# A hybrid attention, state-space and gated-FFN block on one Trainium2 core: the GLU chain rewritten, loads of u split, lists around the down phase reordered

## The reference, cut to what matters

```python
h = rms_norm(x, norm_mix)
q, k, v, u, g = split(h @ w_in)               # 512 | 128 | 128 | 512 | 2 x 1024
a = window_attention(q, k, v, sinks, bias) @ w_attn_branch
y = gelu(Re(C state) + D u)                   # grouped S5 scan over u, 32 groups
b = (y * sigmoid(y @ w_glu + b_glu)) @ w_ssm_branch
x = x + (sigmoid(g_a) * a + sigmoid(g_b) * b) @ w_out
h = rms_norm(x, norm_ffn)
val, gate = split(causal_dwconv(h @ w_up) + conv_b)   # 2 x 2816 columns
x = x + (gelu(gate) * val) @ w_down
return rms_norm(x, norm_final)
```

## Time and profile before

| | |
|---|---|
| time, median of 3 | 2474.99 us |
| the profiled execution | 2474.55 us, span 2472.8 us |
| PE | busy 98% of the span |
| DVE, POOL, ACT | busy 70%, 35%, 30% |
| mean granted TensorE clock | 0.992 of full speed |
| chain that ended last | PE 90%, DVE 5%, DMA 2%, ACT 2%, issue 1% |
| DMA | 367.35 MB, 149 GB/s in the mean |

### The profile page before, as it was taken

How to read it: one execution, slowest core, us unless ns; L and a number is a source line. 1 busy time by engine, 2 the same in 40 slices (tenths; PEclk the granted TensorE clock), 3 DMA queues, 4 the chain that set the end, 5 groups by cost and what they waited for, 6 DMA issues and landing times.

```text
span 2472.8 us, 33390 instructions
## 1 busy us (share of the span) xinstructions
PE 2417.0 (98%) x11578; PEld 1980.7 (80%) x11578; DVE 1737.5 (70%) x2585; ACT 746.4 (30%) x1431; POOL 855.5 (35%) x689
## 2 busy tenths in 40 slices
PE   7999999999999999999999999999999999999997
PEld 6887777888788888788878877778878888888886
DVE  6964564546899999989750346466378888888896
ACT  4145113212333333332221341132133333333222
POOL 2421222450455555623232222235213333334231
PEclk9999999999999999999999999999999999999999
DMA  6266553351334334698522536534312222218863
GB/s 206 77 182 108 175 170 120 133 194 71 102 126 156 135 131 133 216 371 290 183 88 90 104 119 188 158 105 156 148 60 80 91 85 76 78 75 289 311 230 136
DMA packets 178279, 367.35 MB, mean 149 GB/s; under 512 B 22344, under 2 KB 60008, under 8 KB 178168
## 3 DMA queue, kind: packets, MB, share of 16 engines
q1 hardware_dynamic: 135568, 278.23, 34.7%
q10 hardware_dynamic: 42600, 87.64, 10.3%
HBM read 277.20 MB, written 88.60 MB: 148 GB/s over the span
## 4 chain that ended last, share of the span: by engine, by line
PE 90%; DVE 5%; DMA 2%; ACT 2%; issue 1%; POOL 0%; ACTq 0%; SPq 0%; DVEq 0%; POOLq 0%
PE ps L497 28%; PE ps L499 28%; PE ps L498 28%; DMA gates<-junk 1%; PE ps L2220 1%; PE ps L2222 1%; PE ps L2202 1%; DVE ybr_lo L1681 1%; PE ps L2026 1%; PE ps L2074 0%; PE ps L2159 0%; DVE glu_y L1676 0%; ACT ybr_hi L909 0%; DVE z L1809 0%; DVE act_lo L1842 0%
## 5 line engine op out<-in xcount | busy, mean ns | idle before, releaser
L839 POOL CAST slot_hi<-pair_raw 128x512 fp32r<-128x512 f32 x220 | 201.7, 924 | 394.4 <-PE ps L499 305.5
L497 PE MATMUL ps<-act_hi,w_hi 128*128 128x512 f32 x832 | 332.1, 399 | 1.5 <-issue 1.5
L499 PE MATMUL ps<-act_hi,w_lo 128*128 128x512 f32 x832 | 325.4, 391 | 0.0
L498 PE MATMUL ps<-act_lo,w_hi 128*128 128x512 f32 x832 | 324.6, 390 | 0.0
L793 POOL CAST w_hi<-w_raw 128x1024 fp32r<-128x1024 f32 x72 | 80.6, 1119 | 678.4 <-PE ps L499 668.8
L497 PE MATMUL ps<-act_hi,slot_hi 128*128 128x512 f32 x704 | 274.4, 390 | 1.8 <-DVE pre L1795 1.5
L499 PE MATMUL ps<-act_hi,slot_lo 128*128 128x512 f32 x704 | 274.0, 389 | 0.0
L498 PE MATMUL ps<-act_lo,slot_hi 128*128 128x512 f32 x704 | 273.9, 389 | 0.0
L497 PE MATMUL ps<-act_hi 128*128 128x512 f32 x616 | 242.0, 393 | 3.2 <-DVE act_lo L1846 3.2
L498 PE MATMUL ps<-act_lo,act_hi 128*128 128x512 f32 x616 | 240.9, 391 | 0.0
L499 PE MATMUL ps<-act_hi,act_lo 128*128 128x512 f32 x616 | 240.8, 391 | 0.0
(11 more groups left out here) (325 smaller groups left out, 4953.2 us busy)
## 6 DMA issues: line engine op xcount, KB each, us to landing
w_raw<-in_wu SPq DMA_DIRECT2D x88, 512.0 KB, 3.4
pair_raw<-in_wu SPq DMA_DIRECT2D x88, 512.0 KB, 4.1
step_f<-ff SPq DMA_DIRECT2D x88, 512.0 KB, 5.2
ff<-z SPq DMA_DIRECT2D x44, 512.0 KB, 2.6
gates<-junk ACTq DMA_DIRECT2D x64, 256.0 KB, 2.1
sig<-gates ACTq DMA_DIRECT2D x32, 512.0 KB, 5.3
tbl_o<-tables ACTq DMA_DIRECT2D x32, 384.0 KB, 3.6
step_w<-in_wu SPq DMA_DIRECT2D x22, 512.0 KB, 6.8
```

The lines of the kernel that those rows point to most:

```text
L497: nc.tensor.matmul(out, lh, rh, start=first, stop=False, skip_group_check=onto)
L498: nc.tensor.matmul(out, lh, rl, start=False, stop=False, skip_group_check=onto)
L499: return nc.tensor.matmul(out, ll, rh, start=False, stop=last, skip_group_check=onto)
L839: nc.gpsimd.tensor_copy(slot_hi[j][:, :, :], src).then_inc(slot_half[KIND[j]], 1)
```

## The change: what it does

1. GLU: `yT_lo` goes to 160 KiB, where the S5 tables lay, and `ybr_lo` to 112, over `yT`. The value is read from `yT` itself, so the sum (L1674, sixteen in all) is gone. The sigmoid waits for the product that read its buffer, not for `ybr_lo`. All four `y_low` stand behind the last S5 step. The buffers `wo` of the output weights change places to fit.
2. Loads of u: three, three and two transfers, with a pair of weight units behind each group; in block 1 the first group goes ahead of units 14 and 15 and behind 13, in block 0 likewise ahead of 14 and 15.
3. Start of the down phase: DVE interleaves `step_lows` 2, 3, 4 with `near`, `far` and `ff_mul` of the last value; ACT casts step 3 ahead of the last gelu; POOL's last `down_t` stands behind cast 4 instead of cast 2; the last value's store stands ahead of load 10 instead of load 7, and there SP waits for it at once, as before.
4. Between the blocks: in block 0 `bank_add` stands ahead of `out_scaled`; the four output stores move behind the second projection half of block 1; the transposes of the second x half stand ahead of the second product, all but the last two.
5. PE asks for `ybr_lo` before each of the first two S5 products of the merge instead of before the first.

```diff
-        yT_lo = at("yT_lo", 112, [4, T], F32R)
+        yT_lo = at("yT_lo", 160, [4, T], F32R)
-        ybr_lo = at("ybr_lo", 160, [4, T], F32R)
+        ybr_lo = at("ybr_lo", 112, [4, T], F32R)
-              for i, a in enumerate((96, 104, 112, 120, 144, 152, 160, 168))]
+              for i, a in enumerate((96, 104, 160, 168, 112, 120, 144, 152))]
...
-                    if t == 7:
+                    if t == 7 and blk == 0:
+                        down_t(0, FT)
+                    if t == PAIRS_K - 1:
                         store_ff(blk, 0, FT - 1)
-                        if blk == 0:
-                            down_t(0, FT)
                     if t == PAIRS_K - 1:
                         for b in range(2):
                             sp.wait_ge(ff_st[b], 16 * (blk + 1) * (FT // 2))
...
-                load_weights(first, (U_GATE + 6) // 2)
-                load_steps()
+                if blk:
+                    load_weights(first, (U_GATE + 4) // 2)
+                load_steps(0, 3)
+                load_weights((U_GATE + 4) // 2, (U_GATE + 6) // 2)
...
-                load_weights((U_GATE + 6) // 2, (U_GATE + 14) // 2)
+                load_steps(3, 6)
+                load_weights((U_GATE + 6) // 2, (U_GATE + 8) // 2)
+                load_steps(6, STEP)
+                load_weights((U_GATE + 8) // 2, (U_GATE + 14) // 2)
...
-                    if blk == 0 and t == 2:
+                    if blk == 0 and t == 4:
                         down_t(0, FT - 1)
...
+                if blk:
+                    act.wait_ge(step_ready, operands_by(blk - 1, STEPS - 1))
                 copy(kT[:, 0:CH], kprev[:, :])
...
+                    elif n == 2 and blk:
+                        for i in range(HK):
+                            store_out(blk - 1, i)
...
                         if n >= 2:
-                            act.wait_ge(ybr_ready, blk * 8 + n - 1)
+                            act.wait_ge(glu_yr, blk * 8 + n - 1)
...
                 value_hi(2)
+                value_hi(3)
                 gelu(0, FT - 1)
...
-                    if n in (9, 13):
-                        y_low((n - 9) // 4)
...
-                y_low(2)
-                y_low(3)
-
-                dve.wait_ge(y_ready, (blk + 1) * 8)
+                dve.wait_ge(y_done, (blk + 1) * PAIRS)
+                for kt in range(4):
+                    y_low(kt)
...
-                        link(tt(glu_y[b][:, :], f(yT_hi[:, m, cols]), f(yT_lo[:, m, cols]), ALU.add))
                         dve.wait_ge(glu_sig, blk * 8 + n + 1)
-                        tt(glu_y[b][:, :], glu_y[b][:, :], glu_s[b][:, :], ALU.mult).then_inc(glu_yr, 1)
+                        tt(glu_y[b][:, :], yT[:, m, cols], glu_s[b][:, :], ALU.mult).then_inc(glu_yr, 1)
                     if n >= 1:
                         q = n - 1
-                        b, m, cols = q % 2, q // 2, slice((q % 2) * HALF, (q % 2 + 1) * HALF)
+                        b = q % 2
+                        if q % 2 == 0:
+                            dve.wait_ge(glu_yr, blk * 8 + min(q + 2, 8))
...
+                step_lows(2)
                 near(1, 0, FT - 1)
+                step_lows(3)
                 far(1, 0, FT - 1)
-                step_lows(2)
-                ff_mul(0, FT - 1)
-
-                for t in range(3, STEPS):
+                for t in range(4, STEPS):
...
                     step_lows(t)
+                    if t == 4:
+                        ff_mul(0, FT - 1)
...
+                if blk + 1 < BLOCKS:
+                    for q in range(HK):
+                        bank_add(24 + q)
                 dve.wait_ge(gfin_in, 16 * (blk + 1))
                 for i in range(HK):
                     out_scaled(i)
-                for q in range(HK):
+                for q in range(HK if blk + 1 == BLOCKS else 0):
                     bank_add(24 + q)
...
                 for n in (0, 2, 1) + tuple(range(3, 12)):
+                    if n == (2 if blk else 1):
+                        transposes(blk, 1)
                     if n == 1:
-                        transposes(blk, 1)
+                        more_transposes(blk, 1)
                     proj(n)
```

More of the change, by code:

```diff
@@ L747, in load_weights, with load_steps @@
                             load(i + blk * (UNITS // 2), b, i * 2 + b)
-                def load_steps():
+                def load_steps(lo, hi):
                     rows = A["useq"].rearrange("(g c) (t n) -> t c g n", c=SC, t=STEP)
                     sp.wait_ge(u_st, 16 * 4 * (blk + 1))
-                    for t in range(STEP):
+                    for t in range(lo, hi):
                         sp.dma_start(ssT[SC * t:SC * t + SC, :, :], rows[t]).then_inc(steps_in, 16)
-                load_weights(first, (U_GATE + 6) // 2)
-                load_steps()
+                if blk:
+                    load_weights(first, (U_GATE + 4) // 2)
+                load_steps(0, 3)
+                load_weights((U_GATE + 4) // 2, (U_GATE + 6) // 2)
                 def load_y(kt):
@@ L1356, in _ @@
                     transposed_hi(blk + 1, 0, KD - 1, KD)
-                for i in range(HK):
-                    store_out(blk, i)
                 if blk + 1 == BLOCKS:
+                    for i in range(HK):
+                        store_out(blk, i)
                     for i in range(4, TT):
@@ L1982, in _ @@
                     out_scaled(i)
-                for q in range(HK):
+                for q in range(HK if blk + 1 == BLOCKS else 0):
                     bank_add(24 + q)
-                    if blk + 1 == BLOCKS and q:
+                    if q:
                         out_norm(blk, HK + q - 1, HK + q, out_parts(blk) + q)
@@ L2038, in transposes, with more_transposes @@
                             ins.then_inc(tr_done, 1)
+            def more_transposes(blk, h):
                 for k in range(6, KD):
@@ L2088, in _ @@
                     transposes(blk, 0)
+                    more_transposes(blk, 0)
                 def proj(n):
@@ L2244, in _ @@
                     for j in range(2):
-                        if m == 0 and j:
-                            pe.wait_ge(ybr_ready, (blk + 1) * 8)
                         for h in range(2):
+                            if m == 0 and j:
+                                pe.wait_ge(ybr_ready, (blk + 1) * 8)
                             ins = unit_half(4 * (m % 2) + 2 * j + h, m % 2, h, (attn_hi, ybr_hi)[j], (attn_lo, ybr_lo)[j], 4 * j, 4)
```

## The result

The changed kernel takes 2452.35 us (median of four runs, 2451.85 to 2452.94), the kernel before 2474.16 in the runs beside it (2470.70 to 2483.62): ratio 0.9913, 95% interval 0.9895 to 0.9931. The forecast was 2455.5, in a range of 2446 to 2466; it came out 3.2 us too high. The profiled execution of after has a span of 2449.8 us against 2472.8, 23.0 less; the sum had said 19.1.

The account below looks back on a forecast made before the run. The prediction took PE, with its waits and low-clock stretches, to bound the kernel. Its terms, -12.2 - 5.0 - 1.2 - 2.5 - 0.7 + 2.5 = -19.1 on 2474.55, gave 2455.4, stated as 2455.5 us, range 2446 to 2466.

Parts of the forecast that it names:

- Term 1: GLU: wait for `ybr_lo` falls from 5.0 to 1.4 us, 2.43 of low clock goes; 12.2 gained over two blocks.
- the hindrance: GLU's tail: POOL's cast and subtraction and DVE's instructions exclude each other, leaving PE a wait of about 1.4 us.
- rival C: GLU's tail is longer: wait 2.7, clock falls, only 2.3 gained per block, total 2463; chance 0.12.
- Term 2: Loads of u in the attention: gate store lands sooner, PE's wait goes; 5.0 us gained in block 0, 1.2 in block 1.
- Nearer to the case of 3.2 than to that of 13.4: Attention, block 0: gate store's latency comes nearer to 3.2 us (issued before the u loads) than 13.4 (among them).
- The picture of short turns: Attention, block 0: DMA engines alternate between queues packet by packet, so the store's turns are short beside the weight units.
- by about 195: Attention, block 0: time at which the gate store lands, which is the 5.0 us gain.
- rival B: Attention: gate store stays late because DMA time is shared evenly; loads of u gain only 1.2, total 2460.5; chance 0.17.
- Term 3: Between the blocks: PE's waits of 1.5 at the first projection and 1.0 at the transposes go; 2.5 us gained.
- Term 4: Down phase, block 1: step 2's operands stand earlier on DVE; 0.7 us gained with the start-up.
- Term 5: Down phase, block 0: 5.7 gained at step 2, lost in a 5.6 wait at steps 9 and 10; net 2.5 slower.
- rival A: Down phase of block 0 keeps its gain of 5.7 us, total 2447.2; chance 0.18.

Follow-up runs that it names:

- pool_held: Changed kernel with GpSimd's split of the second merge unit held until the last `ybr_lo`; 2450.91 us.
- weights_later: Changed kernel with the pair of weight units between the first two groups of u loads held back in block 0 until the gate store landed; 2460.01 us, one run.
- glu_only: Kernel before with the GLU's part of the change alone; 2457.81 us, ratio 0.9940.
- down_only: Kernel before with only the reordered lists around the down phase and the later store of the last value; 2475.93 us, ratio 1.0005.
- store_early: Changed kernel with the last value's store of block 0 one step earlier, ahead of load 9 instead of load 10; 2449.25 us, ratio 0.9898.
- store_back: Changed kernel with the last value's store of block 0 back in its old place, ahead of `down_t` and load 7; 2456.41 us.
- before_again: Kernel before, unchanged, run and profiled once more; 2474.42 us.
- lows_first: Changed kernel where, in block 0, step 10's operands come ahead of the norm of x and step 11's sums, ACT's rounding ahead of its squares; 2455.60 us.
- u_only: Kernel before with the loads of u in parts and nothing else; 2467.55 us, ratio 0.9983.
- all_three: Changed kernel with store_early, lows_first and pool_held together, plus block 0's first-pass adds one step earlier on DVE; 2445.88 us, ratio 0.9896.

## Why the prediction was right

- **Term 1, the GLU (12.2 said, 13.0 measured).** Right in mechanism and in order. (Its terms, 5.0 + 2.43 - 1.4, add to 6.0 per block, not 6.1.) The remaining wait was 0.7 instead of 1.4 per block. pool_held shows the hindrance that made it; rival C (a tail of 2.7) did not come.
- **Term 2, the loads of u (5.0 and 1.2 said, 5.3 and 1.4 measured).** Right in the sum; the step to it was wrong, so the hit is in part luck. "Nearer to the case of 3.2 than to that of 13.4" is not what happened: 11.0 is nearer to 13.4, and the wait went because 2.4 us were just more than the 2.0 needed. The picture of short turns by which the store would slip through between the weights does not hold either: the store had no turn at all until the weights were nearly done. weights_later shows how thin the margin is: 3 us more, and 3.7 of wait are back. The store's landing "by about 195" meant 9 us, rival B's (time shared evenly) 13; the 11.0 lies half way, and the wait that B kept was gone. Block 1's 1.4 agrees with the 1.2 said, but glu_only has it too without this part.
- **Term 3, between the blocks (2.5 said, 3.2 measured).** Both waits went. The 0.7 more lie in the matmuls round the two waits, which I had put at nothing: each pause between two starts was longer than the idle time that the profile gives for it (1.91 us between starts, where 0.23 is usual, for the wait of 1.52), and some matmuls behind it start slightly apart. The clock was full there, as put.
- **Term 4, the down phase of block 1 (0.7 said, 0.8 measured).** Right.
- **Term 5, the down phase of block 0 (-2.5 said, -1.4 measured).** The riskiest step, and right in mechanism: gain of 5.9 (5.7 said), load 11 at 1085.4 (1085.8), wait 5.3 (5.6), and 1.7 for the slow clock instead of 2.5. Load 7 starts 3.9 us sooner on before's clock (1038.59 in after, with a lead of 12.5, against 1055.04) instead of 2. down_only and store_early confirm the cause, the store in the full queue with SP waiting behind it; rival A is out. The argument also has two gaps that the runs laid open. I weighed the store's new place only as a loss; store_back, where load 7 starts late again, shows it as a gain of 4 us against the old place in the same kernel. And behind the chunk there is a second gate, the adds that step 11 waits for, which the prediction doesn't name: PE waited there 1.7 us in store_early and in before_again, with the old lists, and 8.3 in lows_first. The 5.7 also counts 3.0 for the slow clock behind step 2, which before has in one of its two profiled executions and not in the other.
- **The start.** 0.7 us of the result lie in the first transposes; u_only and lows_first, with the same code there, have a tenth only. It differs from execution to execution and belongs to no edit.

All entries of the table lie within 1.1 us of what was said, and all err to the same side, which makes the 3.9 us of the sum (19.1 against 23.0).

## What to carry to other kernels

When a wait goes, write down who arrives earlier and what stands ready for them: here one repair of the down phase's chunk left 2.3 of 5.3 and brought 1.7 behind it, another left 0 and brought 8.3, and it took the load stream, DVE's order and the place of the adds together to collect the gain. A store on whose landing a queue waits has a best place among the loads: the old one cost 4 us against the new one, and one load earlier than the new one gained 3, with a step's loads going out between the store and the wait for it. One profile is one draw: what a wait costs beyond itself can differ between two executions of the same kernel, here by 2.9 us behind a wait of 2.7 in both. And keep transfers of short runs away from a store on another queue that an engine waits for, since here the store waited for them to drain.

## What the runs showed of the hardware

- Loads of u (16 partitions, runs of 128 elements) keep all 16 DMA engines full at 91 to 104 GB/s (weights_later, 190 to 194; after, 184 to 190). The weights moved at 327 in before (183.6 to 186.4) and, with a little of the store, at 414 in after (191 to 193), with the engines full as well.
- A store on ACT's queue, issued while such loads were under way on SP's, moved no packet for 7.2 us (after), 8.7 (before) or 10.4 (weights_later), then passed in 2 to 4.
- The length of a wait alone did not say whether the low clock follows. In the dense stream of the down phase the granted clock stayed at 1.00 behind 2.28 us in store_early (1074 to 1080), 2.12 in all_three (1086 to 1092) and 2.68 in before_again; it fell to 0.52 behind 2.69 in before, to 0.53 behind 1.93 in store_back (1070 to 1073.4) and to 0.51 behind 5.29 in after (1077.6 to 1081.2). In before's attention, where PE had been doing small products, it was 0.51 behind 2.0.

```profile
1074.00:1080.00 6.00, 5.34 (x24) 4.47 (x25) 5.79 (x12) 0.00 (x0) 1.65 (x2) 1.00 1.04 396
```
```profile
1077.60:1081.20 3.60, 3.56 (x9) 2.83 (x10) 3.44 (x8) 0.00 (x0) 1.65 (x2) 0.51 1.03 402
```
```profile
1070.00:1073.40 3.40, 3.40 (x10) 2.63 (x9) 3.37 (x5) 1.27 (x4) 1.63 (x2) 0.53 1.03 402
```
